# A streaming-encoder layer in fp32: copies of the turned gates without the wait for the spread rows, and the decay work one token tile per later block

## The chip, the cores and the metric

One core of one Trainium2 chip runs the whole program. Its engines are TensorE (PE, with PEld for its weight loads), VectorE (DVE), ScalarE (ACT), GpSimd (POOL) and SyncE (SP), which here only issues transfers. Each engine takes its own instructions in the order in which they are written; they meet only at semaphores. The metric is the time of one execution on the device in microseconds; lower is better.

## The reference, cut to what matters

```python
h = rmsnorm(x, norm1_g)                     # x: 1024 tokens x 1024
z = h @ w_in + b_in                         # 2304 columns and 8 gate columns
aq, ak, av, mq, mk, mv, mo, mi, mf = split(z)
mq, mk = split(silu(causal_dwconv(concat([mq, mk]), w_qk_conv, b_qk_conv)))
att = window_sink_attention(aq, ak, av, sinks)        # 64-token chunks, window of 2
# mLSTM: log_i = mi, cum_f = running sum of log_sigmoid(mf)
d   = cum_f[t] - cum_f[s] + log_i[s]                  # -inf above the diagonal
m_t = maximum(cum_f[t] + m_prev, max_s d)
s_qk = (mq @ mk.T) * exp(d - m_t)                     # exp(d - m_t) is the decay
num  = s_qk @ mv + exp(cum_f + m_prev - m_t) * (mq @ c_prev)
ml   = sigmoid(mo) * num / maximum(|den|, exp(-m_t))
x += concat([rmsnorm(att, g_att), rmsnorm(ml, g_ml)]) @ w_out
x += conv_ffn(rmsnorm(x, norm2_g))                    # 1024 -> 2 x 2816 -> 1024
out = rmsnorm(x, final_g)
```

The kernel keeps the decay as a tile `decay`, 128 partitions (s) by 4 heads by 1024 tokens (t). It is made as exp(min(0, negmax[t] + g[s])), where negmax[t] is a row of the token's running maximum, spread over all partitions, and g[s] a number per partition; then the part above the diagonal is set to zero.

## The kernel before, in words

Every fp32 product is made as three products of rounded parts (`_hi`, `_lo`), and TensorE is meant never to stop. The projection `z = h @ w_in` runs in blocks: the gate columns (block 0), then 18 blocks of 128 columns. Blocks 0 to 3 are made together while x is loaded; `z_block(b)` makes blocks 4 to 18, each of 48 matmuls of 128x128 by 128x512 into one pair of banks, `pz[b % 2]` (L1953, L1949). From block 8 on, `attention(b)` puts pieces of the attention between the two halves of a block: `att_step(block, half)` is the number n of the 64-token chunk whose turn it is, and half a block carries `score(n)`, `attend(n - 3)` and `turn_probs(n - 2)`. At n = -1, which is the start of block 8, it is `turn_values` (L1978): 15 transposes of the value tile into banks 4 to 7.

What feeds a block: SP loads its weights (`load_tile`, L462), ACT rounds them (`weight_high`, L775, which also waits until the block two before is done), DVE takes the remainder (`weight_low`, L1250). What drains it: DVE scales (`z_scale`), ACT adds the bias (`z_keep`). The loops over b in the scalar part (L899) and the vector part (L1469) set the order on these two engines; they run one block behind TensorE's.

The mLSTM gates take a path of their own beside blocks 4 to 7:

1. DVE makes the gate rows, four rows of 1024: `gate_rows(0)` at b = 3 and `gate_rows(1)` at b = 4 (L1308). The steps that matter here are ROW_INTER, ROW_M and, last, ROW_NEGMAX.
2. ACT takes two exponentials of them, `gate_exps` (L825), at b = 5.
3. POOL stores two rows to HBM and loads them again, spread over the partitions: eight transfers, into `decay` and `q_inter` (L721 to L731). Their semaphore is `rows_spread`.
4. Between blocks 6 and 7 TensorE turns the gate rows (L1966 to L1974) into banks 4 and 5. The semaphore is `gates_turned`.
5. DVE copies them out, to `carry` and `gates_t`, and then makes the exponents of the decay, 32 instructions of 128x128: all of it in `decay_args` (L1363), at b = 6, half 1. `gates_t_ready` says that the copies are done; `decay_arg` counts the 32.
6. ACT takes the exponentials, `decay_exps` (L834), eight instructions, at b = 6, half 1, ahead of `weight_high(9)`. POOL zeroes above the diagonal (L733 to L738).

The head of step 5 reads:

```python
dve.wait_ge(s["gates_turned"], 2)
dve.wait_ge(s["rows_spread"], 16 * 8)
```

`turn_values` writes over the banks that hold the turned gates, so it waits for `gates_t_ready` (L1980) besides the value columns (`z_evac`). `score(0)`, at the middle of block 8, waits for `att_v_made`: ACT's four copies of the turned values (`att_v_keep`, L858), which stand behind `weight_high(9)` on ACT. The decay itself is first read by `ml_weigh(0)` (L1445) at n = 20, in block 17 of DVE's loop; `q_inter` is first touched by `scale_q(0)` at n = 8.

Of the kernel before, what the change touches and what calls it, by code (L numbers as in the profile page):

```python
# [5 lines left out]
ALU = mybir.AluOpType  # L6
ACT = mybir.ActivationFunctionType
# [4 lines left out]
P = 128  # L12
# [3 lines left out]
NT = S // P  # L16
# [8 lines left out]
ML_HEADS = 4  # L25
# [93 lines left out]


ATT_BLOCK = 8


def att_step(block, half):

    return 2 * (block - ATT_BLOCK) + half - 1

# [30 lines left out]
def hymba_kernel(nc, x, x_t, w_first, w_tiles, w_gate, vectors, b_in, attn_sinks, w_out, w_up, w_down, final_g, out):  # L158
# [14 lines left out]
    with ExitStack() as ctx:  # L173
        def sb(name, shape, dt=F32):
            return ctx.enter_context(nc.sbuf_tensor(name, shape, dt))

        def sem(name):
            return ctx.enter_context(nc.semaphore(name))
# [4 lines left out]
        def at(slot, name, shape, dt=F32, extra=0):  # L183
            return nc.alloc_sbuf_tensor_at(name, [P, *shape], dt, offset=base + slot * SLOT + extra)
# [103 lines left out]
        decay = at(43, "decay", [ML_HEADS, S])  # L288
# [10 lines left out]
        gates_t = sb("gates_t", [P, 2, NT, ML_HEADS])  # L299
# [64 lines left out]
        s = {n: sem(n) for n in names}  # L364
# [383 lines left out]
        def _(act):  # L748
# [26 lines left out]
            def weight_high(b):  # L775
                act.wait_ge(raw_loaded[b % 3], 16 * ((b - 4) // 3 + 1))
                if b >= 5:
                    act.wait_ge(s["z_done"], 1 if b == 5 else b - 1)
                nc.scalar.activation(w_hi[b % 2][:, :], w_raw[b % 3][:, :], ACT.Copy).then_inc(s["z_hi_made"], 1)
# [51 lines left out]
                nc.scalar.activation(row_a[32:36, :], row_b[0:ML_HEADS, :], ACT.Exp, scale=-1.0)\  # L831
                    .then_inc(s["floor_made"], 1)

            def decay_exps():  # L834
                for i in range(NT):
                    act.wait_ge(s["decay_arg"], ML_HEADS * (i + 1))
                    d = decay[:, :, i * P:(i + 1) * P]
                    nc.scalar.activation(d, d, ACT.Exp).then_inc(s["decay_exp"], 1)

            def silu_qk(n):  # L840

                act.wait_ge(s["qk_tap"], ML_TAPS * (n + 1))
                nc.scalar.activation(z[:, MQ + n, :], qk_acc[:, n % 2, :], ACT.Silu).then_inc(s["qk_made"], 1)
# [14 lines left out]
            def att_v_keep():  # L858

                act.wait_ge(s["att_v_turned"], 1)  # L860
                for c, dst in enumerate((att_va[:, 0:4, :], att_va[:, 4:8, :], att_vb[:, 0:4, :], att_vb[:, 4:7, :])):
                    w = dst.shape[1]
                    last = nc.scalar.activation(dst, bank[4 + c][:, 0:w * P].rearrange("p (n d) -> p n d", n=w),
                                                ACT.Copy)
                last.then_inc(s["att_v_made"], 1)
# [33 lines left out]
            for b in range(FIRST, ZT + 1):  # L899
                if 6 <= b + 2 <= ZT:  # L900
                    weight_high(b + 2)
                if b == ATT_BLOCK - 1:
                    att_v_keep()
                if 0 <= b - WO_BLOCK < NK:
                    wo_high(b - WO_BLOCK)
                for half in range(2):
                    n = att_step(b + 1, half)
                    if half == 1 and b == ATT_BLOCK - 2:
                        decay_exps()
                    if 0 <= n < NC:  # L910
                        att_exps(n)
                    if half == 0:
                        z_keep(b)
                        if b == 5:
                            gate_exps()
                    if 0 <= n - 5 < NC:
                        att_square(n - 5)
                    if n == 20:
                        ml_v_keep(0)
                    if n in (7, 15):  # L920
                        for m in range(2):
                            silu_qk(n // 8 * 2 + m)
# [295 lines left out]
        def _(dve):  # L1218
# [141 lines left out]
                                               in1=z[:, MQ + n, :], op0=ALU.mult, op1=ALU.mult)\  # L1360
                    .then_inc(s["q_inter_made"], 1)

            def decay_args():  # L1363

                dve.wait_ge(s["gates_turned"], 2)
                dve.wait_ge(s["rows_spread"], 16 * 8)
                nc.vector.tensor_copy(carry[:, :, :], bank[5][:, 0:2 * NT].rearrange("p (r i) -> p r i", r=2))
                turned = bank[4][:, 0:NT * 36].rearrange("p (i r) -> p i r", i=NT)
                for n in range(2):
                    last = nc.vector.tensor_copy(gates_t[:, n, :, :], turned[:, :, 32 * n:32 * n + ML_HEADS])  # L1370
                last.then_inc(s["gates_t_ready"], 1)
                dve.wait_ge(s["gates_t_ready"], 1)
                for i in range(NT):
                    for h in range(ML_HEADS):
                        d = decay[:, h, i * P:(i + 1) * P]
                        nc.vector.tensor_scalar(d, d, gates_t[:, 0, i, h:h + 1], 0.0, ALU.add, ALU.min)\
                            .then_inc(s["decay_arg"], 1)
                dve.wait_ge(s["small_loaded"], 48)

                for a in range(2):  # L1380
                    rows = slice(a * 64, (a + 1) * 64)
                    nc.vector.tensor_copy(sink[rows, :], sinks[rows, a:ATT_HEADS:2])
                    last = nc.vector.tensor_scalar(neg_sink[rows, :], sinks[rows, a:ATT_HEADS:2], -1.0, None,
                                                   ALU.mult)
                after(last)


            def att_top(n):
                _, kw = keys(n)
# [79 lines left out]
            for b in range(FIRST, ZT + 1):  # L1469
                for half in range(2):  # L1470
                    n = att_step(b + 1, half)
                    if 0 <= n < NC:
                        att_top(n)
                    if half == 0 and 6 <= b + 2 <= ZT:
                        weight_low(b + 2)
                    if half == 0:
                        z_scale(b)
                    if 0 <= n - 2 < NC:
                        att_p_keep(n - 2)
                    if 0 <= n - 3 < NC:  # L1480
                        att_keep(n - 3)
                    if half == 0 and b in (3, 4):
                        gate_rows(b - 3)
                    if half == 1 and b == ATT_BLOCK - 2:
                        decay_args()
                    if half == 1 and 0 <= b - WO_BLOCK < NK:
                        wo_low(b - WO_BLOCK)
                    if 0 <= n < NC:
                        att_sum(n)
                    if 0 <= n < 4 * ML_TAPS:  # L1490
                        conv_tap(n)
                    if n in (8, 10):
                        scale_q((n - 8) // 2)
                    if n == 19:
                        ml_ones()
                    if n == 20:
                        ml_weigh(0)
# [377 lines left out]
        def _(pe):  # L1875
# [278 lines left out]

            for b in range(ATT_BLOCK, ZT + 1):
                z_block(b, attention(b))
# [143 lines left out]
```

## Time and profile before

| what | value |
|---|---|
| median of 3 runs | 1040.54 us (1038.54 to 1041.67) |
| the profiled execution | 1041.56 us, its span 1039.8 us |
| PE busy | 1013.7 us (97%), 4863 matmuls |
| DVE busy | 742.2 us (71%) |
| ACT busy | 499.9 us (48%) |
| POOL busy | 30.2 us (3%) |
| chain that ended last | PE 85%, DVE 5%, DMA 4%, ACT 2% |

The page cuts the span into 40 slices of 26 us and shows for each the busy share of an engine in tenths. TensorE reads 9 nearly everywhere, and 5 and 8 in the slices from 78 to 130 us. The views used below are the table of waits (who waited for whom, and how long), the timelines of single engines (start, length, instruction, and in brackets the idle time before it with what ended it), the instructions of one line, and the transfers with their time from issue to landing.

### The profile page before, as it was taken

How to read it: one execution, taken by the hardware profiler on the slowest of the kernel's cores; microseconds unless marked ns; L12 is line 12 of the kernel's file. 1: busy time of each engine (PE TensorE's matmuls, PEld its weight loads, DVE VectorE, ACT ScalarE, POOL GpSimd, SP SyncE). 2: the span in 40 equal slices, each digit the busy share in tenths (PEclk: the TensorE clock that was granted, in tenths of full speed). 3: DMA queues.
4: the chain of work that ended last, by engine and by line, in shares of the span. 5: the costliest groups of instructions: out<-in, count | busy, mean ns of one | idle time of the engine just before them, and what ended most of it. 6: DMA issues, size and time to landing. Idle time of an engine off the chain costs nothing.

```text
span 1039.8 us, 13151 instructions
## 1 busy us (share of the span) xinstructions
PE 1013.7 (97%) x4863; PEld 838.0 (81%) x4863; DVE 742.2 (71%) x1159; ACT 499.9 (48%) x931; POOL 30.2 (3%) x50
## 2 busy tenths in 40 slices
PE   9995899999999999999999999999999999999997
PEld 7884788888888888878888888888888888888886
DVE  5370766763475557998777777777777788995796
ACT  5640546444452323665445454454454644444573
POOL 2001200000120000000000000000000000000000
PEclk9998899999999999999999999999999999999999
DMA  9317143430652224233132231231230999035104
GB/s 344 127 40 204 61 149 124 153 122 1 237 170 81 81 81 129 75 116 107 61 102 82 81 102 62 81 101 61 84 100 21 369 358 376 30 96 191 48 1 163
DMA packets 94929, 129.26 MB, mean 124 GB/s; under 512 B 5768, under 2 KB 60168, under 8 KB 94864
## 3 DMA queue, kind: packets, MB, share of 16 engines
q1 hardware_dynamic: 93520, 125.07, 35.7%
q0 software_dynamic: 1056, 3.18, 1.4%
q8 instruction: 39, 0.64, 0.3%
q14 instruction: 26, 0.21, 0.1%
q10 hardware_dynamic: 288, 0.15, 0.1%
HBM read 100.04 MB, written 28.35 MB: 123 GB/s over the span
## 4 chain that ended last, share of the span: by engine, by line
PE 85%; DVE 5%; DMA 4%; ACT 2%; SPq 1%; issue 1%; POOL 0%; DVEq 0%; ACTq 0%
PE pz L1949 11%; PE pz L2211 7%; PE pz L2212 7%; PE pz L2213 7%; PE pd L2211 6%; PE pd L2212 6%; PE pd L2213 6%; PE pd L2232 4%; PE pd L2234 4%; PE pd L2235 4%; PE pz L2232 3%; PE pz L2234 3%; PE pz L2235 3%; PE pd L2142 3%; PE pd L2140 3%; PE pd L2141 3%
## 5 line engine op out<-in xcount | busy, mean ns | idle before, releaser
L1048 ACT ACTIVATE ws_hi<-raw 128x512 fp32r<-128x512 f32 x88 | 52.9, 626 | 103.7 <-PE pz L2213 48.0
L2211 PE MATMUL pz<-ht_hi,ws_hi 128*128 128x512 f32 x240 | 93.7, 390 | 1.0 <-DVE u L1691 0.8
L2213 PE MATMUL pz<-ht_hi,ws_lo 128*128 128x512 f32 x240 | 93.4, 389 | 0.0
L2212 PE MATMUL pz<-ht_lo,ws_hi 128*128 128x512 f32 x240 | 93.4, 389 | 0.0
L2211 PE MATMUL pd<-ht_hi,ws_hi 128*128 128x512 f32 x200 | 77.8, 389 | 0.0
L2212 PE MATMUL pd<-ht_lo,ws_hi 128*128 128x512 f32 x200 | 77.8, 389 | 0.0
L2213 PE MATMUL pd<-ht_hi,ws_lo 128*128 128x512 f32 x200 | 77.8, 389 | 0.0
L1949 PE MATMUL pz<-h_hi,w_hi 128*128 128x512 f32 x240 | 77.0, 402 | 0.0
L1949 PE MATMUL pz<-h_lo,w_hi 128*128 128x512 f32 x240 | 75.2, 395 | 0.0
L1949 PE MATMUL pz<-h_hi,w_lo 128*128 128x512 f32 x240 | 74.6, 392 | 0.0
L1708 DVE SCALAR_TENSOR_TENSOR gate<-u,vec,gate 128x1023 f32<-128x1023 f32 (+1 forms) x44 | 56.5, 1284 | 19.4 <-ACT gate L1090 18.6
L1678 DVE TENSOR_TENSOR ws_lo<-raw,ws_hi 128x512 fp32r<-128x512 f32 x88 | 58.6, 687 | 0.7 <-ACT ws_hi L1048 0.7
L1708 DVE SCALAR_TENSOR_TENSOR lift<-u,vec,lift 128x1023 f32<-128x1023 f32 (+1 forms) x44 | 56.2, 1278 | 0.1
L2211 PEld LDWEIGHTS pz<-ht_hi,ws_hi 128*128 128x128 f32 x240 | 45.0, 188 | 11.7 <-issue 1.9
L1123 ACT ACTIVATE d_hi<-a 128x512 fp32r<-128x512 f32 x44 | 27.7, 630 | 54.5 <-PE pd L2235 29.5
L1949 PEld LDWEIGHTS pz<-h_hi,w_lo 128*128 128x128 f32 x240 | 45.6, 190 | 10.1
L1949 PEld LDWEIGHTS pz<-h_lo,w_hi 128*128 128x128 f32 x240 | 45.6, 190 | 9.9
L2213 PEld LDWEIGHTS pz<-ht_hi,ws_lo 128*128 128x128 f32 x240 | 45.0, 188 | 9.4
L2212 PEld LDWEIGHTS pz<-ht_lo,ws_hi 128*128 128x128 f32 x240 | 45.1, 188 | 9.2
L2232 PE MATMUL pd<-d_hi,d_hi 128*128 128x512 f32 x132 | 51.3, 389 | 0.0
L2234 PE MATMUL pd<-d_lo,d_hi 128*128 128x512 f32 x132 | 51.3, 389 | 0.0
L2235 PE MATMUL pd<-d_hi,d_lo 128*128 128x512 f32 x132 | 51.3, 389 | 0.0
(305 smaller groups left out, 2474.7 us busy)
## 6 DMA issues: line engine op xcount, KB each, us to landing
raw<-in_w_up SPq DMA_DIRECT2D x48, 512.0 KB, 4.8
b<-in_w_down SPq DMA_DIRECT2D x49, 256.0 KB, 7.0
act_rows<-gate SPq DMA_DIRECT2D x22, 512.0 KB, 2.6
a<-act_rows SPq DMA_DIRECT2D x44, 256.0 KB, 4.6
w_raw<-in_w_tiles SPq DMA_DIRECT2D x15, 512.0 KB, 4.5
x_turned<-in_x_t SPq DMA_DIRECT2D x8, 512.0 KB, 9.2
x_in<-in_x SPq DMA_DIRECT2D x8, 512.0 KB, 12.8
wo_hi_rows<-wo_new_hi SPq DMA_DIRECT2D x8, 512.0 KB, 2.6
```

Of the source, the lines that this page charges most:

```text
L1048: nc.scalar.activation(ws_hi[m][:, :, :], summand(p, i), ACT.Copy).then_inc(s["ws_hi_made"], 1)
L1678: nc.vector.tensor_tensor(ws_lo[m][:, :, :], summand(p, i), ws_hi[m][:, :, :].bitcast(F32), ALU.subtract)\
L1708: nc.vector.scalar_tensor_tensor(out=dst[:, back:], in0=src[:, 0:S - back], scalar=w, in1=dst[:, back:], op0=ALU.mult, op1=ALU.add).then_i ...
L1949: ins = mm(dst[:, h * HALF:(h + 1) * HALF], w[:, c], h_part(part, k, h), start=first, stop=last)
L2140: mm(bank[4 + n % 4], mix_hi[u][:, k, :], wo_hi[:, k, c], start=k == 0, stop=False)
L2141: mm(bank[4 + n % 4], mix_hi[u][:, k, :], wo_lo[:, k, c], start=False, stop=False)
L2211: mm(dst, wh[:, k, :], xh[:, k, :], start=begins and k == 0, stop=False, skip_group_check=not begins)
L2212: mm(dst, wh[:, k, :], xl[:, k, :], start=False, stop=False, skip_group_check=not begins)
L2213: ins = mm(dst, wl[:, k, :], xh[:, k, :], start=False, stop=k == KH - 1, skip_group_check=not begins)
L2232: mm(dst, d_hi[m, 0][:, c], d_hi[m, 1][:, :], start=begins and k == 0, stop=False, skip_group_check=not begins)
L2234: mm(dst, d_hi[m, 0][:, c], d_lo[m, 1][:, :], start=False, stop=False, skip_group_check=not begins)
L2235: ins = mm(dst, d_lo[m, 0][:, c], d_hi[m, 1][:, :], start=False, stop=k == KT - 1, skip_group_check=not begins)
```

## The change

- DVE, b = 6, half 1: `decay_args` becomes `gates_keep`. It waits for `gates_turned` alone, makes the three copies and the four small sink instructions, and no decay.
- DVE, blocks b = 9 to 16, half 0: `decay_args(b - 9)` makes the four exponents of one token tile. The first of them waits for `rows_spread`.
- ACT: `decay_exps`, eight instructions at b = 6, becomes `decay_exp(i)`, one instruction at half 1 of blocks 9 to 16.
- ACT: `gate_exps` is done at b = 4 in place of b = 5.
- PE, SP and POOL keep their programs. POOL's steps follow the semaphores that ACT now raises at other times.

```diff
+DECAY_BLOCK = 9
@@ scalar part
-            def decay_exps():
-                for i in range(NT):
-                    act.wait_ge(s["decay_arg"], ML_HEADS * (i + 1))
-                    d = decay[:, :, i * P:(i + 1) * P]
-                    nc.scalar.activation(d, d, ACT.Exp).then_inc(s["decay_exp"], 1)
+            def decay_exp(i):
+                act.wait_ge(s["decay_arg"], ML_HEADS * (i + 1))
+                d = decay[:, :, i * P:(i + 1) * P]
+                nc.scalar.activation(d, d, ACT.Exp).then_inc(s["decay_exp"], 1)
...
-                    if half == 1 and b == ATT_BLOCK - 2:
-                        decay_exps()
+                    if half == 1 and 0 <= b - DECAY_BLOCK < NT:
+                        decay_exp(b - DECAY_BLOCK)
...
-                        if b == 5:
+                        if b == 4:
                             gate_exps()
@@ vector part
-            def decay_args():
+            def gates_keep():
                 dve.wait_ge(s["gates_turned"], 2)
-                dve.wait_ge(s["rows_spread"], 16 * 8)
                 nc.vector.tensor_copy(carry[:, :, :], ...)
                 ...
                 last.then_inc(s["gates_t_ready"], 1)
-                dve.wait_ge(s["gates_t_ready"], 1)
-                for i in range(NT):
-                    for h in range(ML_HEADS):
-                        ...
+            def decay_args(i):
+                if i == 0:
+                    dve.wait_ge(s["gates_t_ready"], 1)
+                    dve.wait_ge(s["rows_spread"], 16 * 8)
+                for h in range(ML_HEADS):
+                    d = decay[:, h, i * P:(i + 1) * P]
+                    nc.vector.tensor_scalar(d, d, gates_t[:, 0, i, h:h + 1], 0.0, ALU.add, ALU.min)\
+                        .then_inc(s["decay_arg"], 1)
...
                     if half == 1 and b == ATT_BLOCK - 2:
-                        decay_args()
+                        gates_keep()
+                    if half == 0 and 0 <= b - DECAY_BLOCK < NT:
+                        decay_args(b - DECAY_BLOCK)
```

The program order of DVE around b = 6 before; `w_lo` is the remainder of a block's weights, and the waits stand in brackets:

```order
L1289 TENSOR_TENSOR z<-pz,rstd_row 128x1024 [waits z_done]
L1367 COPY carry<-pd 128x16 [waits rows_spread,gates_turned]
L1370 COPY gates_t<-pd 128x32 x2
L1376 TENSOR_SCALAR decay<-decay,gates_t 128x128 [waits gates_t_ready]
L1376 TENSOR_SCALAR decay<-decay,gates_t 128x128 x31
L1382 COPY sink<-sinks 64x4 [waits small_loaded]
```

The same place of DVE's program now:

```order
L1289 TENSOR_TENSOR z<-pz,rstd_row 128x1024 [waits z_done]
L1366 COPY carry<-pd 128x16 [waits gates_turned]
L1369 COPY gates_t<-pd 128x32 x2
L1375 COPY sink<-sinks 64x4 [waits small_loaded]
L1376 TENSOR_SCALAR neg_sink<-sinks 64x4
```

The copies have lost the wait on `rows_spread`, and nothing of the decay follows them here.

ACT's program over the same blocks before, where `w_hi` is the rounded weights, L828 and L831 are `gate_exps`, L838 `decay_exps` and L863 the copies of the turned values:

```order
L812 ACTIVATE zq<-zq,vec 128x16x64 [waits z_scaled]
L779 ACTIVATE w_hi_266<-w_raw_260 128x1024 [waits z_done,raw_loaded1]
L812 ACTIVATE z<-z,vec 128x1024 [waits z_scaled]
L828 ACT_TABLE_LOAD
L828 ACTIVATE row_c<-row_c 4x1024 [waits row_step]
L831 ACTIVATE row_a<-row_b 4x1024 [waits row_step]
L779 ACTIVATE w_hi_265<-w_raw_261 128x1024 [waits z_done,raw_loaded2]
L812 ACTIVATE z<-z,vec 128x1024 [waits z_scaled]
L838 ACTIVATE decay<-decay 128x4x128 [waits decay_arg] x8
L779 ACTIVATE w_hi_266<-w_raw_259 128x1024 [waits z_done,raw_loaded0]
L863 ACTIVATE att_va<-pd 128x512 [waits att_v_turned]
```

And now:

```order
L813 ACTIVATE zq<-zq,vec 128x16x64 [waits z_scaled]
L829 ACT_TABLE_LOAD
L829 ACTIVATE row_c<-row_c 4x1024 [waits row_step]
L832 ACTIVATE row_a<-row_b 4x1024 [waits row_step]
L780 ACTIVATE w_hi_266<-w_raw_260 128x1024 [waits z_done,raw_loaded1]
L813 ACTIVATE z<-z,vec 128x1024 [waits z_scaled]
L780 ACTIVATE w_hi_265<-w_raw_261 128x1024 [waits z_done,raw_loaded2]
L813 ACTIVATE z<-z,vec 128x1024 [waits z_scaled]
L780 ACTIVATE w_hi_266<-w_raw_259 128x1024 [waits z_done,raw_loaded0]
L863 ACTIVATE att_va<-pd 128x512 [waits att_v_turned]
```

The two gate exponentials have moved ahead of block 7's `w_hi`, and the eight exponentials of the decay are gone from in front of block 9's.

DVE's program in block 9, half 0, now, where the first tile of the decay stands:

```order
L1422 COPY probs_t<-pd 128x512 [waits att_p_turned]
L1428 TENSOR_TENSOR zq<-pd,inv 128x256 [waits att_summed,att_done]
L1387 TENSOR_SCALAR decay<-decay,gates_t 128x128 [waits rows_spread,gates_t_ready]
L1387 TENSOR_SCALAR decay<-decay,gates_t 128x128 x3
L1409 TENSOR_TENSOR total<-total,sink_e 128x4 [waits att_exped]
```

Four exponents stand between what TensorE's next half needs and the chunk's own sums; seven more such groups follow, one to a block.

ACT's program in blocks 15 and 16 now, where exponentials, SiLU (L843) and sigmoid (L813) alternate:

```order
L813 ACT_TABLE_LOAD
L813 ACTIVATE z<-z,vec 128x1024
L873 ACTIVATE att_squares,sq_att<-zq 128x256
L843 ACT_TABLE_LOAD
L843 ACTIVATE z<-qk_acc 128x1024 x2
L838 ACT_TABLE_LOAD
L838 ACTIVATE decay<-decay 128x4x128
L873 ACTIVATE att_squares,sq_att<-zq 128x256
L780 ACTIVATE w_hi_265<-w_raw_259 128x1024
L813 ACT_TABLE_LOAD
```

From here to block 17 the program now has six table loads, where it had three.

## Rows read from the trace of the kernel before

**Rows 1.** The page: granted TensorE clock in tenths, 40 slices of the span.
```profile
PEclk9998899999999999999999999999999999999999
```

**Rows 2.** Waits of PE: who waited for whom, us in total, times, longest.
```profile
PE pd L1983 <- DVE gates_t L1370: 13.2, 1, 13.2
PE pd L1996 <- ACT att_vb L863: 2.5, 1, 2.5
```

**Rows 3.** Timeline of PE from the end of block 7: start, length, instruction.
```profile
91.04 0.61 PE L1949 MATMUL pz<-h_hi,w_lo 128*128 128x512 f32 x2
...
104.86 3.43 PE L1983 MATMUL pd<-ident,z 128*128 128x128 f32 x15 [13.20 <-DVE gates_t L1370]
107.94 1.20 PE L1949 MATMUL pz<-h_hi,w_hi 128*128 128x512 f32 x2
...
114.28 0.61 PE L1949 MATMUL pz<-h_hi,w_lo 128*128 128x512 f32 x2
117.36 1.06 PE L1996 MATMUL pd<-z,zq 64*128 64x64 f32 x8 [2.47 <-ACT att_vb L863]
...
125.18 0.71 PE L1996 MATMUL pd<-z,zq 64*128 64x128 f32 x8
...
131.49 0.72 PE L1996 MATMUL pd<-z,zq 64*128 64x128 f32 x8
132.14 0.63 PE L2007 MATMUL pd<-ident,probs 128*64 128x128 f32 x4
132.53 0.70 PE L1949 MATMUL pz<-h_hi,w_hi 128*128 128x512 f32 x2
...
138.17 0.71 PE L1996 MATMUL pd<-z,zq 64*128 64x128 f32 x8
```

**Rows 4.** Timeline of DVE: the last gate row, the first copy.
```profile
70.62 0.68 DVE L1336 TENSOR_SCALAR row_d<-row_d 4x1024 f32<-4x1024 f32 x1
...
104.05 0.17 DVE L1367 COPY carry<-pd 128x16 f32<-128x16 f32 x1 [21.09 <-DMA q_inter<-inter_rows]
```

**Rows 5.** Timeline of ACT, blocks 7 to 9, and a wait in a later block.
```profile
68.62 1.06 ACT L779 ACTIVATE w_hi<-w_raw 128x1024 fp32r<-128x1024 f32 x1 [1.72 <-PE pz L1949]
...
74.90 1.28 ACT L828 ACT_TABLE_LOAD   x1
...
82.98 1.15 ACT L812 ACTIVATE z<-z,vec 128x1024 f32<-128x1024 f32 x1 [2.43 <-DVE z L1289]
...
114.42 1.04 ACT L779 ACTIVATE w_hi<-w_raw 128x1024 fp32r<-128x1024 f32 x1
...
116.33 0.98 ACT L863 ACTIVATE att_vb<-pd 128x512 f32<-128x512 f32 x2
...
163.21 0.37 ACT L853 ACTIVATE probs<-pd,neg_top 128x128 f32<-128x128 f32 x1 [4.13 <-PE pd L2007]
```

**Rows 6.** Timeline of POOL: first store of a row, first spreading transfer.
```profile
77.54 0.55 POOL L722 DMA_DIRECT2D inter_rows<-row_c  x1 [38.16 <-ACT row_c L828]
...
80.57 0.56 POOL L728 DMA_DIRECT2D decay<-negmax_rows  x1 [1.95 <-DMA negmax_rows<-row_d]
```

**Rows 7.** Timeline of SP: block 9's weights issued.
```profile
81.86 0.58 SPq L465 DMA_DIRECT2D w_raw<-in_w_tiles  x1
```

**Rows 8.** The same transfer: KB, and us from issue to landing.
```profile
w_raw<-in_w_tiles SPq DMA_DIRECT2D x1, 512.0 KB, 11.3
```

**Rows 9.** Instructions on the tile decay: ns min/median/max; times to landing of its transfers.
```profile
L1376 DVE TENSOR_SCALAR decay<-decay,gates_t x32: 272/274/756, 104.7 to 113.6; 128x128 f32<-128x128 f32 x32
...
L838 ACT ACTIVATE decay<-decay x8: 629/632/635, 105.7 to 113.9; 128x512 f32<-128x512 f32 x8
L736 POOL TENSOR_SCALAR_AFFINE_SELECT decay<-decay x8: 630/634/700, 106.4 to 114.6; 128x512 f32<-128x512 f32 x8
...
DMA to landing us min/median/max: 6.3/12.7/18.6
```

**Rows 10.** Timeline of DVE in a later block: idle time ahead of a score's maximum.
```profile
176.90 0.76 DVE L1394 TENSOR_REDUCE top<-pd 128x2 f32<-128x256 f32 x2 [1.75 <-PE pd L1996]
```

More of the change, by code:

```diff
@@ L1371, in decay_args @@
                 last.then_inc(s["gates_t_ready"], 1)
-                dve.wait_ge(s["gates_t_ready"], 1)
-                for i in range(NT):
-                    for h in range(ML_HEADS):
-                        d = decay[:, h, i * P:(i + 1) * P]
-                        nc.vector.tensor_scalar(d, d, gates_t[:, 0, i, h:h + 1], 0.0, ALU.add, ALU.min)\
-                            .then_inc(s["decay_arg"], 1)
                 dve.wait_ge(s["small_loaded"], 48)
```

## The prediction

> **What bounds the kernel now.** I read four views in this order.
>
> The waits of PE came first. TensorE is busy for 97% of the span, so only what stops or slows TensorE can be won back. Two waits stand out [rows 2]: 13.2 us for DVE's copies of the turned gates and 2.5 us for ACT's copies of the turned values. Both lie in block 8. The clock line of the page has its only 8s in the two slices around this place [rows 1]: TensorE was also slowed there.
>
> The timeline of PE gives the place. The last pair of matmuls of block 7 starts at 91.04 and is over at 91.66. The value transposes start at 104.86. The score of chunk 0 is held until 117.36 [rows 3].
>
> The timeline of DVE gives the cause of the first wait. DVE stands for 21.09 us, so from 82.96, and what ends this is the last spreading transfer, at 104.05 [rows 4]. The gates are turned between blocks 6 and 7; a block is two halves of about 5.6 us (below), so that was near 91.7 - 11.2 = 80.5. So the copies waited only for rows that they do not read.
>
> The timeline of ACT gives the cause of the second. Block 9's `w_hi` begins at 114.42, straight after the eighth decay exponential (the first of the eight starts at 105.7, the last at 113.9 [rows 9]). The copies of the values follow it and end at 117.31, and PE resumes at 117.36 [rows 3, 5].
>
> **The change part by part.**
>
> *The copies without the wait.* DVE is free at 82.96 and the gates are turned, so the copies and the four small sink instructions should be over within two or three us, near 85. `turn_values` also needs the value columns, which ACT finishes at 84.13 [rows 5]. TensorE comes there at 91.66, more than 6 us later. The wait of 13.20 us goes to nothing.
>
> *The exponentials out of ACT's way.* ACT now comes to block 9's `w_hi` with nothing before it. That instruction needs block 7 done (91.7) and block 9's weights landed. They were issued at 81.86 and took 11.3 us, so 93.2 [rows 7, 8]. From the start of `w_hi` to the end of the value copies it took 117.31 - 114.42 = 2.89 us [rows 5], so the copies end at 93.2 + 2.9 = 96.1. TensorE wants them at 91.6 + 1.5 (transposes) + 5.6 (half a block) = 98.7. The wait of 2.47 us goes too, with 2.6 us to spare. This is the tightest margin of the plan: what is late next is block 9's weights.
>
> *The clock.* After the long wait, and again after the short one, matmuls ran slowly: the first pair took 1.20 us where the last pair of block 7 took 0.61, and the half behind the short wait took longer than the same half a chunk later [rows 3]. That is the lower of the two clock levels, 1.2 GHz in place of 2.4. With no wait the clock should stay up. The pieces, by starts in [rows 3]:
> - 15 transposes: 107.94 - 104.86 = 3.08 us. Four transposes at full clock took 132.53 - 132.14 = 0.39, so 15 take 1.47. Won: 1.61.
> - First half of block 8: 107.94 to the end of the pair at 114.28, 114.89, is 6.95. A half at full clock is 138.17 - 132.53 = 5.64. Won: 1.31.
> - Score of chunk 0 and second half: 125.18 - 117.36 = 7.82, against 131.49 - 125.18 = 6.31 at full clock. Won: 1.51.
>
> Sum: 13.20 + 2.47 + 1.61 + 1.31 + 1.51 = 20.1 us. Everything behind this place is TensorE working without a pause, and its feeders are tied to TensorE's own progress by semaphores, so the rest of the program moves forward as a whole.
>
> The Trainium skill ("TensorE: Matmul & The Clock Gate", section "What's actually happening") says that the throttled clock is the default and that activity releases it. The slow matmuls right behind both waits agree with it. If the clock did not depend on the waits, the sum would be 15.7.
>
> *`gate_exps` at b = 4.* ACT now comes to it before its rows are made, loads the table, and waits for DVE. The row for the second exponential is ready just before 70.62 [rows 4], so both are done by 71.7. Queued behind them is block 7's `w_hi`, which started at 68.62 [rows 5]: it now ends near 71.7 + 1.1 = 72.8. DVE's remainder of these weights and one scaling follow. They would have to take over 7 us together to reach TensorE, which starts block 7 at 80.5. The delay costs nothing. The gain is on POOL: its first store can start at 70.7 to 71.4 in place of 77.54, so the first spreading transfer starts near 74 in place of 80.57 [rows 6], and the last lands near 97 in place of 104.
>
> *Decay exponents on DVE.* 32 of them, from 104.7 to 113.6 + 0.3, took some 9.1 us [rows 9], 0.285 us each, so four take 1.14 us in each of blocks 9 to 16. They stand behind all that TensorE's next half needs. Behind them are the chunk's sums, read three steps later, and one convolution tap. DVE is idle for 1.75 us before the next chunk's maximum [rows 10], and this repeats in every block there. So 0.6 us is left and TensorE sees nothing. Were this cover gone, it would cost up to 1.14 us x 8 = 9.1.
>
> *The wait for the rows.* It now stands in block 9, half 0, ahead of the sums and of the next maximum. The chunk of that half had its score at 138.17 [rows 3], now near 118, and DVE comes there later still. The rows are there by 104 even at the old pace: 14 us to spare, no cost.
>
> *Decay exponentials on ACT and the zeroing on POOL.* One of 0.63 us for each block [rows 9], where ACT is idle for 4.13 us before a chunk's exponentials [rows 5]. In blocks 15 to 17 ACT has three more table loads of 1.28 us [rows 5], in a stretch where it waits for TensorE every block: hidden. POOL has nothing else to do there. The last tile is finished in block 16 and the first is read in block 17.
>
> *SP.* Nothing is moved. Its store and load of the output weights hang on DVE's `wo_low(0)`, which now comes some 19 us earlier, as TensorE does.
>
> The sum is made against the profiled execution: 1041.56 - 20.1 = 1021.4. That execution was 1.0 us above the median of the runs, so on the scale of the median it is 1040.54 - 20.1 = 1020.4.
>
> **The rivals.**
>
> *B. Block 9's weights are late.* They share the transfer engines with the spreading rows. For it: 11.3 us to land. Against: the rows now start 6 us earlier, so less of them is left beside it. Lower bound of the landing: the 11.3 us of before or less, no cost. Upper bound: the slowest transfer of this stretch, 18.6 us [rows 9]. It would land at 100.5, the value copies would end at 103.4, and TensorE would wait 4.7 us at the score and then run one half slowly (1.5): 6.2 us, so 1026.6. I take the lower bound, since it is the same transfer at the same time.
>
> *C. DVE is sometimes late in a block.* A few tenths of a us, in some of eight blocks: 1021 to 1025. For it: only 0.6 us left. Against: a late maximum reaches TensorE only through ACT's exponentials, and TensorE asks for those half a block later, over 6 us after the score.
>
> *D. The decay work holds up every block (slower than before).* Each exponent takes the longest of its 32 times, 0.756 us, and one zeroing of 0.63 us on POOL holds DVE as well [rows 9]: 4 x 0.756 + 0.63 = 3.65 us a block, less 1.75 of cover, is 1.90, times 8 is 15.2. If every pause lowers the clock for half a block as the one of 2.47 us did, 1.18 us more each, that is 9.4. Together 24.6, which is 4.5 us more than is won: 1045.0. It decides from 20.1 / 8 = 2.5 us a block on TensorE. For it: the spread between 274 and 756 ns. Against: the median is at the minimum, and a pause has to come through ACT first.
>
> The Trainium skill ("SBUF — State Buffer", on the shared port pair) says that a GpSimd instruction and a DVE instruction that needs the shared ports exclude each other for a whole instruction, which speaks against putting the zeroing beside a busy DVE. The trace agrees: single exponents of up to 756 ns beside a median of 274 fall where POOL's zeroing runs, and the 9.1 us for 32 hold these already. By this rule each block has one hold of at most 0.63 us, now on another DVE instruction, and the time is that of the forecast or of C.
>
> *E. The change does not do what it says.* If the copies waited for something else that also came at 104, nothing would move: 1040.5. Against: DVE resumes with the landing of the last row, and the turned gates were 23 us old.
>
> **How the numbers follow.** The forecast, 1020.4 (own range 1018.4 to 1022.4), gets 0.85; B 0.08; C 0.03; D 0.02; E 0.02. The range reaches down by the spread of the runs and up into B and C: 1018 to 1024. About 0.3% (3 us) is what a measurement of this kernel can tell from no change. Faster is the forecast, B and C: 0.96. Same is E, 0.02; slower is D, 0.02.
>
> **What the changed profile would show.** Right: no wait of PE above 1.5 us; value transposes starting near 91.6 and taking about 1.5 us; the score of chunk 0 near 98.7; the clock line without its 8s; DVE's copies near 83; the first spreading transfer near 74; DVE idle before the maxima reduced to about 0.6 us after a decay group. Wrong: PE waiting at the score of chunk 0 for the value copies (B), with block 9's `w_hi` ended by a transfer; PE waits in blocks 9 to 16 for exponentials or probabilities (C, D); the copies on DVE still ended by a transfer (E).

## The result, and the profile after

| | before | after |
|---|---|---|
| median of the runs | 1040.34 us (1038.54 to 1041.67) | 1023.55 us (1022.3 to 1027.02) |
| the profiled execution | 1041.56 us, span 1039.8 | 1022.62 us, span 1020.9 |
| PE busy | 97% | 99% |

The ratio is 0.9845 (95% interval 0.9815 to 0.9875). The kernel is faster, as forecast, by 16.8 us in the medians where 20.1 was forecast. By the ratio, the median of 1040.54 from which the prediction set out becomes 1024.4, just above its range of 1018 to 1024. In two later series of runs the same kernel gave 1022.08 us (ratio 0.982, 0.9806 to 0.9835) and 1022.58 us (0.9832, 0.9816 to 0.9848), inside the range. Against the forecast of 1020.4, the three medians lie 1.7 to 3.2 us too high, and the ratio of the first series puts the distance at 4.0.

The page after: the clock line, which had its 8s in [rows 1].

```profile
PEclk9999999999999999999999999999999999999999
```

The waits of PE after, in place of [rows 2] (columns as there: us in total, times, longest):

```profile
PE pd L1908 <- POOL idle_data L683: 1.4, 1, 1.4
PE pd L2000 <- ACT att_vb L863: 1.1, 1, 1.1
PE pz L2215 <- DVE u L1695: 0.8, 1, 0.8
```

The wait for the gates is gone. The wait for the value copies (L863) is still there, smaller: 1.1 us in place of 2.5. The other two stand at the start of the program and in the FFN and were there before.

The timeline of PE after, the same place as [rows 3]:

```profile
91.15 0.62 PE L1953 MATMUL pz<-h_hi,w_lo 128*128 128x512 f32 x2
91.61 1.80 PE L1987 MATMUL pd<-ident,z 128*128 128x128 f32 x15
93.16 0.70 PE L1953 MATMUL pz<-h_hi,w_hi 128*128 128x512 f32 x2
...
98.28 0.61 PE L1953 MATMUL pz<-h_hi,w_lo 128*128 128x512 f32 x2
99.95 0.66 PE L2000 MATMUL pd<-z,zq 64*128 64x64 f32 x8 [1.06 <-ACT att_vb L863]
...
106.21 0.72 PE L2000 MATMUL pd<-z,zq 64*128 64x128 f32 x8
```

Before, chunk 1's score started at 125.18, and now at 106.21: 18.97 us earlier, of the 18.9 by which the span is shorter. So nothing is won or lost behind this place. The reader can see how near the sum of 20.1 was: 18.97 + 1.06 for the wait that stayed + 0.11 by which block 7 ended later (91.15 against 91.04) is 20.14.

Why there is still a wait is in the timeline of ACT after, in place of [rows 5]:

```profile
97.00 1.06 ACT L780 ACTIVATE w_hi<-w_raw 128x1024 fp32r<-128x1024 f32 x1 [12.76 <-DMA w_raw<-in_w_tiles]
97.97 1.06 ACT L863 ACTIVATE att_va<-pd 128x512 f32<-128x512 f32 x2
98.92 0.98 ACT L863 ACTIVATE att_vb<-pd 128x512 f32<-128x512 f32 x2
```

ACT stood for 12.76 us for block 9's weights. The transfers of that stretch, issued at 81.96, in place of [rows 8]:

```profile
w_raw<-in_w_tiles SPq DMA_DIRECT2D x1, 512.0 KB, 15.0
```

They took 15.0 us to land, in place of 11.3, although the spreading rows now start 6 us earlier. POOL's timeline, in place of [rows 6]:

```profile
71.12 0.68 POOL L723 DMA_DIRECT2D inter_rows<-row_c  x1 [31.34 <-ACT row_c L829]
...
74.35 0.56 POOL L729 DMA_DIRECT2D decay<-negmax_rows  x1 [1.83 <-DMA negmax_rows<-row_d]
```

The two transfer queues show what happened (packets, MB, and the time of their packets as a share of the 16 transfer engines, which can add up to a little over 100%; q0 carries POOL's rows, q1 what SP issues). After, from 82 to 86 us:

```profile
q0 software_dynamic: 252, 0.90, 101.4%
```

There is no line for q1: of SP's five transfers that were issued from 80.73 on, nothing was moved until 86. Before, where both queues were given their work at the same moment (80.6), they shared the engines: 72.4% for q0 and 21.8% for q1 from 82 to 86 us, and then, from 86 to 90 us:

```profile
q1 hardware_dynamic: 170, 0.62, 54.1%
q0 software_dynamic: 153, 0.57, 47.5%
```

So rows with a head start kept the engines to themselves for a while, and what SP issued behind them waited. In windows of a quarter of a microsecond, SP's first packet shows about 3.2 us behind its first issue in the kernel before and about 5.6 us behind it here. The Trainium skill ("DMA: Bandwidth & Descriptors", section "Queues, rings and completion order") says that each transfer engine takes turns between the queues that have work for it. The rows of before from 86 on agree with that. The 4 us of after do not, counted from the moment of issue, and here the measurement decides; the profile does not show when SP's work reached the engines, so whether the rule itself fails stays open.

### The profile page after: what moved, and what is told of

It is laid out like the page before. It is cut to its first block, busy times and chain, and to the rows that moved or that the text cites. A ratio compares the mean times of both kernels' runs of the same rounds, so it can differ in the third digit from the quotient of the medians.

```text
span 1020.9 us, 13154 instructions
## 1 busy us (share of the span) xinstructions
PE 1009.5 (99%) x4863; PEld 834.8 (82%) x4863; DVE 738.5 (72%) x1159; ACT 503.4 (49%) x934; POOL 34.0 (3%) x50
## 4 chain that ended last, share of the span: by engine, by line
PE 94%; DVE 3%; DMA 1%; ACT 1%; issue 0%; SPq 0%; POOL 0%; DVEq 0%; POOLq 0%
PE pz L1953 15%; PE pz L2215 7%; PE pz L2216 7%; PE pz L2217 7%; PE pd L2215 6%; PE pd L2217 6%; PE pd L2216 6%; PE pd L2236 4%; PE pd L2238 4%; PE pd L2239 4%; PE pz L2236 3%; PE pz L2238 3%; PE pz L2239 3%; PE pd L2146 3%; PE pd L2144 3%; PE pd L2145 3%
```

## The experiments

The theory T: the distance to the sum is the wait for block 9's weights, whose landing differs from run to run. The rival R: it lies in the later blocks, with the decay work. Where a difference of less than 1 us is read, the two kernels ran on the same chip in turn.

### The changed kernel again

No edit.

> The changed kernel itself, once more, for its spread and a second trace. Theory T (block 9's weights, issued behind the rows' backlog on the shared transfer engines, land late and by a varying amount): median 1022 to 1025, single runs from 1022 to 1027; TensorE waits 1 us or more at the score of chunk 0, ended by the value copies, and ACT's w_hi of block 9 is ended by its transfer at about 97. Rival R (the missing 1 to 3 us lie in the later blocks, with the decay work): the same median, but the wait at chunk 0 explains less than half of the distance to 1020.4 and other waits or slower halves show in blocks 9 to 16.

Measured: 1022.08 us (1021.93 to 1022.26). ACT's `w_hi` of block 9 started at 96.26, ended by its transfer, and TensorE waited 0.7 us:

```profile
99.21 0.66 PE L2000 MATMUL pd<-z,zq 64*128 64x64 f32 x8 [0.66 <-ACT att_vb L863]
```

The place is T's, though the wait is shorter than the 1 us that T asked for, and the runs are closer together than expected. One sign of R did come: the wait of 0.66 us is less than half of the 1.7 us by which this median lies above 1020.4. The other sign of R did not: no wait shows in blocks 9 to 16. Where the remaining 1.0 us comes from is taken up below.

### Block 9's weights first

```diff
             for b in range(7, ZT + 1):
-                load_tile(b)
+                if b != 9:
+                    load_tile(b)
+                if b == 8:
+                    load_tile(9)
```

> The changed kernel with one edit: block 9's weights are issued as soon as block 6 is done, ahead of the first two output-weight pieces. T: they land by about 91 in place of 97, the wait at the score of chunk 0 is gone, median 1020.5 to 1022 and single runs closer together. R: nothing changes, 1022 to 1025.

Measured: 1021.35 us (1021.13 to 1022.24), 0.7 less than the changed kernel. Its trace has no wait at the score of chunk 0. The weights landed 11.6 us after their issue at 80.30, and ACT no longer waited for them but for TensorE's block 7:

```profile
92.62 1.06 ACT L783 ACTIVATE w_hi<-w_raw 128x1024 fp32r<-128x1024 f32 x1 [7.62 <-PE pz L1956]
```

Here too nothing of SP's moved before 86, although the weights were first in its queue. They landed at 91.9 in place of 97.0, with nothing of SP's ahead of them. The profiled execution was the slowest of its runs, 1022.24, and was late before this place: it came to the turning of the gates at 80.20, against 79.44 and 79.10 in the two traces of the changed kernel. So the start of the program scatters by about 1 us. T had also said that the runs would lie closer together than the changed kernel's, and they do not.

### The gate exponentials back at b = 5

```diff
-                        if b == 4:
+                        if b == 5:
                             gate_exps()
```

> The changed kernel with the gate exponentials back at b = 5, so that the spreading rows are issued from 80.6 as before. T: block 9's weights land near 93, as in the kernel before, the wait at chunk 0 is gone, median 1020.5 to 1022.5: this part of the change then costs time. R: no difference from the changed kernel. A third view (the transfer engines are shared evenly, so starting the rows early helps): slower than the changed kernel, 1024 to 1027.

Measured: 1021.58 us (1021.38 to 1021.87), 0.5 less than the changed kernel, and no run overlaps with its runs. Block 9's weights took 11.2 us, as before the change, and ACT went on at 93.03:

```profile
93.03 1.06 ACT L780 ACTIVATE w_hi<-w_raw 128x1024 fp32r<-128x1024 f32 x1 [8.92 <-DMA w_raw<-in_w_tiles]
```

So moving the exponentials, which was meant to bring the rows early, costs the changed kernel 0.5 us in this series. My third view, that the engines are shared evenly, is refuted: it is the one on which the prediction rested.

### Both edits

The two edits above together: block 9's weights first and the gate exponentials at b = 5.

> Both edits: block 9's weights first and the gate exponentials at b = 5. T: the weights are issued near 79.4, ahead of the rows, and land near 83; no wait at chunk 0, median 1020.5 to 1022. R: 1022 to 1025.

Measured: 1021.39 us (1021.21 to 1021.75). The weights took 3.4 us to land, and TensorE has no wait in block 8.

### One part of the change alone: the copies

The exponents and exponentials of the decay go back to b = 6; the copies keep their shorter wait.

```diff
                     if half == 1 and b == ATT_BLOCK - 2:
                         gates_keep()
-                    if half == 0 and 0 <= b - DECAY_BLOCK < NT:
-                        decay_args(b - DECAY_BLOCK)
+                        for i in range(NT):
+                            decay_args(i)
...
-                    if half == 1 and 0 <= b - DECAY_BLOCK < NT:
-                        decay_exp(b - DECAY_BLOCK)
+                    if half == 1 and b == ATT_BLOCK - 2:
+                        for i in range(NT):
+                            decay_exp(i)
```

> The changed kernel with the decay work put back where it was: all 32 exponents on DVE and all eight exponentials on ACT at b = 6, behind the wait for the rows; only the copies keep their new, shorter wait. T (two waits in a row, the second one ACT's): the value transposes start at 91.6, but ACT comes to block 9's weights only after the eighth exponential, near 107, so TensorE stands at the score of chunk 0 from 98.7 to about 110: 11 to 12 us and 1 to 3 us of lowered clock, 1034 to 1037. Rival (the copies alone bring the gain): 1021 to 1023.

Measured: 1033.32 us (1033.09 to 1034.36), ratio to before 0.9924 (0.9906 to 0.9941). One long wait in place of two:

```profile
108.79 1.12 PE L2001 MATMUL pd<-z,zq 64*128 64x64 f32 x8 [9.28 <-ACT att_vb L863]
...
117.01 0.71 PE L2001 MATMUL pd<-z,zq 64*128 64x128 f32 x8
```

The mechanism is T's, but the median lies below the 1034 to 1037 that were expected. The wait is 9.3 us and not 11 to 12, because ACT came to the weights at 105.86 and not 107, and because TensorE came to the score 0.7 us later than said (99.5 against 98.7). From one score to the next it took 8.22 us in place of 6.26: 2.0 us for the clock.

### One part of the change alone: the spread decay work

```diff
                 dve.wait_ge(s["gates_turned"], 2)
+                dve.wait_ge(s["rows_spread"], 16 * 8)
```

> The changed kernel with the wait for the rows back in front of the copies; the decay work stays spread over blocks 9 to 16. T: the copies wait for the rows, which now land near 97, so TensorE stands 5 to 7 us at the value transposes and then runs 3 to 5 us slower on a lowered clock; the second wait is gone: 1029 to 1034. Rival (DVE's copies are needed by nobody before the decay exponents): 1021 to 1023.

Measured: 1029.01 us (1028.37 to 1031.14), ratio to before 0.9884 (0.986 to 0.9908). TensorE waits at the value transposes, now for the rows alone:

```profile
97.73 3.43 PE L1988 MATMUL pd<-ident,z 128*128 128x128 f32 x15 [6.08 <-DVE gates_t L1370]
106.64 0.66 PE L2001 MATMUL pd<-z,zq 64*128 64x64 f32 x8
```

From the transposes to the score it took 8.91 us, against 7.28 in the changed kernel without interruption (91.61 to 98.89): 1.6 us for the clock, where 3 to 5 were expected.

Each part alone leaves one of the two waits: the copies alone win 8.2 us, the spreading alone 12.5 (medians of the same series of runs, before at 1041.53). Both have the earlier exponentials. The rows are still waited for in both, so these should help here; no run without them was made.

### Block 9's weights one place further back

```diff
             for b in range(7, ZT + 1):
-                load_tile(b)
+                if b != 9:
+                    load_tile(b)
...
                     load_wo(b - WO_BLOCK - 1)
+                if b == 9:
+                    load_tile(9)
```

> The changed kernel with block 9's weights issued after the next output-weight piece, 0.5 MB further back. T: they land 2 to 3 us later (99 to 100), the wait at the score of chunk 0 grows from 0.7 or 1.1 us to 3 to 4 us, and the clock falls for half a block, 1 to 1.5 us more: 1025 to 1027, which is where the slowest run of the changed kernel was. R (landing doesn't set the time): 1022.

Measured: 1022.66 us (1021.54 to 1025.18). The expectation of 1025 to 1027 was missed, and the profiled execution (1021.54) had no wait at all. The weights, issued behind 84.15, let ACT go on at 95.10:

```profile
95.10 1.06 ACT L783 ACTIVATE w_hi<-w_raw 128x1024 fp32r<-128x1024 f32 x1 [10.83 <-DMA w_raw<-in_w_tiles]
```

In this execution the rows moved faster. From 82 to 86 us, against 0.90 MB in the changed kernel:

```profile
q0 software_dynamic: 306, 1.11, 99.4%
```

So the order of issue does not set the landing alone; how fast the rows ahead move counts as well, and that differs between executions. What the slower runs waited for is not shown. Single runs of this kernel were 1021.54, 1022.02, 1023.3 and 1025.18 us, with mean granted clocks of 0.999, 0.999, 0.998 and 0.997.

### Block 9's weights only behind the last row

```diff
             def load_tile(b):
                 if b >= 7:
                     sp.wait_ge(s["z_done"], b - 2)
+                if b == 9:
+                    sp.wait_ge(s["rows_spread"], 16 * 8)
```

> The changed kernel with block 9's weights issued only when all spread rows have landed (near 92 to 97), so that they land near 97 to 101. T: TensorE stands at the score of chunk 0 by as much as the landing is past 95.8, up to 5 us, and with a wait of 2 us or more the clock falls for half a block and costs 1 to 2 us more: 1023 to 1028, and the trace shows landing, wait and clock together. R: 1022.

Measured: 1022.28 us (1021.79 to 1027.25). The median misses the expectation of 1023 to 1028 and is where R had put it; three of the four runs show no sign of a late landing. That the rows were quick in those three is likely, but there is no trace of them. The fourth run, which is the profiled one, has 1027.25 us and a mean granted clock of 0.995, and shows the whole mechanism. The weights were issued at 94.98, when the last row had landed, and took 3.7 us. The timelines of ACT and PE in it:

```profile
98.67 1.06 ACT L782 ACTIVATE w_hi<-w_raw 128x1024 fp32r<-128x1024 f32 x1 [14.34 <-DMA w_raw<-in_w_tiles]
...
101.62 1.12 PE L2002 MATMUL pd<-z,zq 64*128 64x64 f32 x8 [2.64 <-ACT att_vb L865]
102.67 1.22 PE L1955 MATMUL pz<-h_hi,w_hi 128*128 128x512 f32 x2
...
110.80 0.72 PE L2002 MATMUL pd<-z,zq 64*128 64x128 f32 x8
```

The busy times of its stages, with the granted clock as the third figure from the end (then the share of the transfer engines, and GB/s):

```profile
101.60:104.00 2.40, 2.38 (x11) 2.07 (x12) 1.73 (x6) 2.33 (x4) 0.00 (x0) 0.50 0.00 0
104.00:106.00 2.00, 2.00 (x6) 1.52 (x6) 1.64 (x4) 1.09 (x9) 0.00 (x0) 0.50 0.15 61
106.00:108.00 2.00, 2.00 (x7) 1.52 (x6) 0.27 (x1) 0.00 (x0) 0.00 (x0) 0.52 1.02 401
108.00:110.00 2.00, 2.00 (x10) 1.65 (x9) 0.00 (x0) 0.00 (x0) 0.00 (x0) 1.00 0.20 68
```

Weights 1.7 us later than in the changed kernel (98.67 against 97.00) make the wait 2.64 us in place of 1.06. Behind the longer wait the clock stands at 0.50 for 6 us, and from score to score it takes 110.80 - 101.62 = 9.18 us in place of 6.26: 2.92 us lost. Wait and clock are 5.6 us, and 1027.25 - 5.6 = 1021.7 is the time without them. The slowest run of the changed kernel in the first series, 1027.02 us at a clock of 0.995, reads just like this one. That it had this wait is argued from those two numbers; there is no trace of it.

### The changed kernel and the one with both edits, side by side again

> The changed kernel a third time, beside the next one on the same chip. T (block 9's weights land late by an amount that differs from run to run, as the spreading rows ahead of them move at 210 to 275 GB/s): median 1022 to 1024, single runs 1 to 5 us apart, the longer ones with the lower granted clock.

> Block 9's weights issued first and the gate exponentials at b = 5, on this chip. T: the weights land near 83, 12 us before they can hold anything up, so both the wait and the scatter are gone: 1021 to 1022, single runs within 1 us. R (the scatter is the chip's or lies in later stages): as scattered as the changed kernel.

Measured: 1022.58 us (1022.04 to 1023.59) and 1021.76 us (1021.1 to 1022.25). The changed kernel's profiled execution had its weights just in time and no wait at the score; it is the fastest of its runs, 1022.04.

```profile
95.88 1.06 ACT L780 ACTIVATE w_hi<-w_raw 128x1024 fp32r<-128x1024 f32 x1 [11.10 <-DMA w_raw<-in_w_tiles]
```

With both edits the landing is out of the matter: ACT's `w_hi` is ended by TensorE's own block 7 and not by a transfer.

```profile
91.43 1.06 ACT L783 ACTIVATE w_hi<-w_raw 128x1024 fp32r<-128x1024 f32 x1 [7.62 <-PE pz L1956]
```

In the medians the kernel with both edits is 0.7 us faster than the changed one in the first of the two series, where no run of one overlaps with a run of the other, and 0.8 us in the second, where they overlap. It is level with the one that only has block 9's weights first (1021.39 and 1021.35). The two profiled executions of the second series differ by 0.9 us although neither waits: the transposes start at 92.14 in one and at 91.17 in the other, so that difference is the scatter of the start. The runs with both edits span 1.15 us here, where less than 1 was expected, against 1.55 for the changed kernel.

### The price of DVE's cover

```diff
+                for r in range(3):
+                    nc.vector.tensor_reduce(junk_d[:, 3 * i + r:3 * i + r + 1], rstd_row[:, :], AX_X, ALU.max)
                 for h in range(ML_HEADS):
                     d = decay[:, h, i * P:(i + 1) * P]
```

`junk_d` is a spare tile. On the changed kernel:

> The changed kernel with three extra DVE instructions in front of each of the eight decay groups, a maximum over a row tile of 1024 elements that nobody reads, 1.1 us each. It asks for the price of DVE's cover in blocks 9 to 16. T: a late maximum reaches TensorE only through ACT's exponentials, which have 3 us or more in hand, so 3.3 us more on DVE in every second half costs 0 to 1 us in all: 1022 to 1023. Rival D of the prediction (what DVE is late by, TensorE waits for in each block): 3.3 + 0.9 - 1.75 = 2.4 us a block, 19 us in all and more with the clock: 1041 or above.

Measured: 1024.86 us (1022.7 to 1026.62). The median lies above the expectation. The profiled execution (1023.27) has 1.4 us of wait for the value copies in it, so the scatter of the weights is mixed in; what the two runs of over 1026 us waited for is not shown. The kernel with both edits takes the weights out:

> The kernel with both edits plus the three extra 1.1 us DVE instructions in front of each decay group: the price of DVE's cover without the scatter of the weights. T: 0.4 to 1 us above the kernel with both edits, so 1021.8 to 1022.5. Rival D: 10 us or more above it.

Measured: 1022.05 us (1021.91 to 1022.37), 0.3 above the kernel with both edits in the same series. Its trace shows on DVE the extra work, the decay group, and no idle time left before the next maximum:

```profile
123.50 3.46 DVE L1390 TENSOR_REDUCE junk_d<-rstd_row 128x1 f32<-128x1024 f32 x3
126.88 0.86 DVE L1393 TENSOR_SCALAR decay<-decay,gates_t 128x128 f32<-128x128 f32 x4
...
129.18 0.75 DVE L1402 TENSOR_REDUCE top<-pd 128x2 f32<-128x256 f32 x2
```

and on PE what comes of it in all eight blocks, a single new row in its waits:

```profile
PE pd L2006 <- ACT sink_e L860: 0.4, 2, 0.2
```

3.46 us a block, 28 us of DVE work, cost TensorE 0.4 us. Rival D, which asked for 10 us or more, is refuted. R falls too: five times the DVE work of the decay itself, in the same blocks, costs less than what R had to explain.

## Why the prediction was right and where it was wrong

*The copies without the wait: right.* The value transposes start at 91.61 (said: 91.6), and DVE's copies at 82.97:

```profile
82.97 0.16 DVE L1366 COPY carry<-pd 128x16 f32<-128x16 f32 x1
```

*The clock: right in each piece of block 8.* The transposes take 93.16 - 91.61 = 1.55 us (said: 1.47), the first half 98.89 - 93.16 = 5.73 (5.64), score and second half 6.26 (6.31).

*The exponentials out of ACT's way: the mechanism was right, one term was wrong.* The step that failed reads "they were issued at 81.86 and took 11.3 us, so 93.2", and under rival B "the rows now start 6 us earlier, so less of them is left beside it". I took a transfer time from one arrangement of the queues into another. With a head start of the rows the same transfer took 15.0 us and landed at 97.0, and the margin of 2.6 us was gone. It cost 1.06 us in the profiled execution, 0.66 and nothing in two others, and with clock 5.6 where it was forced late. With the exponentials back at b = 5, and nothing else changed, the transfer took 11.2 us again and the wait was gone: that shows the cause.

*`gate_exps` at b = 4: right in its times, wrong in its verdict.* POOL's first store came at 71.12 (said: 70.7 to 71.4), the first spreading transfer at 74.35 (said: near 74), and block 7 was not held up. But it was given as costing nothing and costs 0.5 us. The queue behind it that I did not ask about was SP's.

*From the profiled execution to the median: wrong by 1.0 us, and the second step that failed.* The sum against the profiled execution was 1021.4; I then subtracted the 1.0 us by which that execution lay above the median, and so came to 1020.4. That takes the distance as scatter of the whole program, which stays when a wait goes. But the scatter of before seems to have lain mostly in the waits that went: before's runs span 5.1 us in one series (1038.06 to 1043.16, clocks of 0.992 and 0.988 at the ends), and those of the kernel with both edits beside them 0.54 us (1021.21 to 1021.75). No trace of a fast and a slow run of before shows where they differ, so this is argued from the spans. Without any wait in block 8 the kernel runs at 1021.39 and 1021.76, which is the sum of 1021.4 without the subtraction.

With these two steps the distance of 3.2 us in the medians of the first series comes to this: 1.0 us for the subtraction, 1.2 us in the profiled execution (1.06 us of wait and 0.11 from an earlier place), and 0.9 us by which the median lies above that execution, through two slower runs (1024.47 and 1027.02) of which there is no trace. That they too waited for the weights is likely and not shown.

*Rival B: the right rival, too cheap and too unlikely.* It was given 0.08 and happened, in small, in two of three profiled executions of the changed kernel. Its price for the clock was the 1.5 us that followed the wait of 2.47 us of before; a wait of 2.64 us was followed by 2.9. With what these runs showed, the forecast would have been 1021.4 plus 0 to 1.1 us in most executions and up to 5.6 in some, with the upper end of the range at 1027.

*Decay work in the later blocks, C and D: right.* Four exponents take 0.86 us, less than the 1.14 said, and DVE keeps 0.9 to 1.0 us of idle time before the next maximum, where 0.6 was said ([rows 10] had 1.75). The price of D had a slip: the text takes 1.18 us of clock for each pause, "as the one of 2.47 us did", but that one cost 1.51 by its own sum, so D stood at about 1048 and not 1045.0. Nothing hangs on it, as no such pause came.

The first such place:

```profile
124.23 0.86 DVE L1387 TENSOR_SCALAR decay<-decay,gates_t 128x128 f32<-128x128 f32 x4
...
127.51 0.76 DVE L1396 TENSOR_REDUCE top<-pd 128x2 f32<-128x256 f32 x2 [0.89 <-PE pd L2000]
```

The three more table loads of ACT are there, 1.28 us each, and nobody waits for them.

*E: refuted.* The copies did what the change says, as their start at 82.97 shows.

Open stays why the transfer engines served only POOL's queue for 4 us. The five other traces read with the rows some 6 us ahead (the changed kernel twice more, and the three with block 9's weights first, one place back, or behind the rows) show the same: SP's first packet came between 85.8 and 87.7 us, 5 to 6.5 us behind its first issue. No experiment varied the length of the head start, so no rule for it is given.

## What to carry to other kernels

When a wait on the critical path is taken away, the next thing in line is often a transfer with a few microseconds in hand; its time has to be read again for the new order of issue, not copied from the old trace, and a load that something depends on should be issued ahead of bulk traffic that nobody needs yet. A wait that goes can take its scatter with it, so a sum made from one profiled execution need not be shifted by that execution's distance to the median. Two waits in a row have to be removed together: here each part alone left the other one standing at 6 to 9 us.

## What the runs showed of the hardware that I had not expected

Two queues that were filled at the same time shared the transfer engines, with 72.4% and 21.8% in the first 4 us and about evenly after that (54.1% and 47.5%). Where POOL's queue had a head start of 6 us, it had 101.4% for 4 us and SP's issued transfers none.

Waits of TensorE of 0.66, 1.06 and 1.40 us left the granted clock at 1.00 (the last one in the changed kernel with the three extra DVE instructions). Waits of 2.47 and 2.64 us were each followed by a stretch near 0.50 (0.53 to 0.55 and 0.50 to 0.52 in windows of about 2 us), and the second cost nearly twice the first (2.9 against 1.5 us), at nearly the same length. Behind the longer ones the clock cost 1.6 us (wait of 6.08), 2.0 (9.28) and 2.9 (13.20). In these five the price of the clock did not follow the length of the wait.

POOL's zeroing instructions became longer. [rows 9] had 634 ns in the middle; the instructions on the tile `decay` after:

```profile
L1387 DVE TENSOR_SCALAR decay<-decay,gates_t x32: 274/278/282, 124.2 to 229.8; 128x128 f32<-128x128 f32 x32
...
L737 POOL TENSOR_SCALAR_AFFINE_SELECT decay<-decay x8: 634/1271/1454, 125.8 to 232.0; 128x512 f32<-128x512 f32 x8
```

The exponents no longer have a time above 282 ns, and it is POOL's instructions that take longer: the first zeroing, 1.27 us from 125.84, lies beside a DVE tap with two operands from 125.37 to 126.62. This fits the shared port that the prediction weighed, now with POOL as the one that is held; that the port is the cause is argued from the times. Spreading the work moved this price from DVE to POOL, where it costs nothing.
